# Two-layer hybrid streaming encoder on one core: attention weights of units 2 to 7 turned by VectorE blocks and a round trip through DRAM instead of by TensorE

## What is computed

```python
def swa_mixer(p, sinks, cos, sin):
    q, k, v = split_cols(p, (4 * 64, 2 * 64, 2 * 64))
    ...
    kb, vb = band(kr, km), band(vr, vm)          # 16 meta keys, the previous chunk, the own chunk
    ...
    pr = sink_softmax(jnp.einsum('bcqkgd,bcskd->bckgqs', qr, kb), sink, valid)
    orr = jnp.einsum('bckgqs,bcskd->bcqkgd', pr.astype(v.dtype), vb)
```

## Time and profile before

| | |
|---|---|
| runs | 3054.97, 3055.97, 3060.37 us; median 3055.97 |
| profiled execution, its own time | 3056.32 us |
| span of its trace | 3054.4 us |
| PE busy | 3011.8 us, 99% of the span |
| DVE, ACT, POOL busy | 1529.4, 939.6, 216.8 us |
| DMA | 760.19 MB, mean 249 GB/s |

### The profile page before, as it was taken

The page is one execution under the profiler, slowest core; times in us unless marked ns, Lnnn a source line. Parts: engine busy times, 40 slices in busy tenths (PEclk is TensorE's granted clock), DMA queues, the critical chain, the costliest instruction groups (busy, mean ns, idle before and its releaser), DMA issues.

```text
span 3054.4 us, 64343 instructions
## 1 busy us (share of the span) xinstructions
PE 3011.8 (99%) x27180; PEld 2759.9 (90%) x27180; DVE 1529.4 (50%) x3672; ACT 939.6 (31%) x2381; POOL 216.8 (7%) x319
## 2 busy tenths in 40 slices
PE   8999999999999999999999999999999999999998
PEld 7788778889898899989989899999999999999998
DVE  4345552355633455336554366544566255663562
ACT  3324440134421343124341144303343043421320
POOL 0111010011101110010010101000000000000000
PEclk9999999999999999999999999999999999999999
DMA  7577477788978989888797898986768857787887
GB/s 256 170 205 213 118 208 218 220 237 283 311 236 263 280 273 320 242 259 272 238 313 210 264 276 261 295 284 196 260 205 268 290 178 249 210 267 253 301 302 248
DMA packets 227116, 760.19 MB, mean 249 GB/s; under 512 B 25088, under 2 KB 44672, under 8 KB 226576
## 3 DMA queue, kind: packets, MB, share of 16 engines
q1 hardware_dynamic: 189328, 620.80, 61.6%
q0 software_dynamic: 37504, 135.28, 18.0%
HBM read 744.33 MB, written 136.31 MB: 288 GB/s over the span
## 4 chain that ended last, share of the span: by engine, by line
PE 92%; DMA 3%; DVE 3%; ACT 2%; issue 0%; SPq 0%; ACTq 0%; DVEq 0%
PE psum L1853 29%; PE psum L1306 27%; PE psum L1876 10%; PE psum L1912 8%; PE psum L1443 7%; DMA slots<-in_weights 2%; PE psum L1300 1%; PE psum L1322 1%; PE psum L1621 1%; PE psum L1646 1%; DMA slots<-wsum 1%; PE psum L1633 1%; PE psum L1572 1%; PE psum L1694 1%; PE psum L1803 1%
## 5 line engine op out<-in xcount | busy, mean ns | idle before, releaser
L1306 PE MATMUL psum<-hT,slots 128*128 128x256 f32 (+1 forms) x2880 | 658.9, 387 | 2.8 <-ACT hT L874 2.1
L1306 PEld LDWEIGHTS psum<-hT,slots 128*128 128x128 f32 x2880 | 541.6, 190 | 97.0 <-issue 5.5
L1853 PE MATMUL psum<-tsum,slots 128*128 128x128 f32 (+1 forms) x4928 | 608.0, 277 | 11.6 <-ACT raw L1223 4.9
L1853 PEld LDWEIGHTS psum<-tsum,slots 128*128 128x128 f32 x4928 | 573.1, 191 | 28.6 <-issue 20.2
L1853 PE MATMUL psum<-hT,slots 128*128 128x128 f32 (+1 forms) x3696 | 453.7, 276 | 6.9 <-DMA slots<-in_weights 3.9
L1853 PEld LDWEIGHTS psum<-hT,slots 128*128 128x128 f32 x3696 | 432.6, 192 | 10.1 <-DMA slots<-in_weights 4.9
L1876 PE MATMUL psum<-gT,slots 128*128 128x256 f32 (+1 forms) x1408 | 309.9, 383 | 0.0
L1876 PEld LDWEIGHTS psum<-gT,slots 128*128 128x128 f32 x1408 | 267.1, 190 | 40.9
L1306 PE MATMUL psum<-mixT,slots 128*128 128x256 f32 (+2 forms) x1024 | 226.4, 381 | 1.1 <-DVE hT L2030 1.1
L1306 PEld LDWEIGHTS psum<-mixT,slots 128*128 128x128 f32 x1024 | 194.3, 190 | 29.7 <-issue 1.5
L2030 DVE SCALAR_TENSOR_TENSOR hT<-hT,psum 128x256 f32<-128x256 f32 (+2 forms) x96 | 40.5, 423 | 348.3 <-PE psum L1876 249.7
(11 more groups left out here) (326 smaller groups left out, 3526.6 us busy)
## 6 DMA issues: line engine op xcount, KB each, us to landing
slots<-in_weights SPq DMA_DIRECT2D x667, 512.0 KB, 4.6
slots<-wsum SPq DMA_DIRECT2D x308, 512.0 KB, 4.5
wsum<-in_weights POOLq DMA_DIRECT2D x132, 512.0 KB, 6.7
slots<-wsumi SPq DMA_DIRECT2D x64, 512.0 KB, 4.4
slots<-wsumd SPq DMA_DIRECT2D x64, 512.0 KB, 4.5
wsum<-wsum POOLq DMA_DIRECT2D x44, 512.0 KB, 7.9
wsumi<-in_weights POOLq DMA_DIRECT2D x24, 512.0 KB, 7.5
wsumd<-in_weights POOLq DMA_DIRECT2D x24, 512.0 KB, 9.3
```

Of the source, the lines that this page charges most:

```text
L1306: ins = mm(psum[:, i % 2, :n], lhsT, rhs, start=k == 0, stop=k == len(pairs) - 1)
L1853: ins = mm(dst[:, e * n:(e + 1) * n], w[:, (4 * e + k) * P:(4 * e + k + 1) * P], moving[s][k], start=s in (0, 1, 5) and e == 0 and k == 0, ...
```

## The change

For tiles of 128 queries in units 2 to 7 (`weights_by_blocks`: twelve tiles) TensorE's transposes and ACT's two copies of them are gone. In their place:

- DVE, in the step of the normalisation, turns the weights in blocks of 32 by 32 (`v.transpose`, two instructions, L2669) from `PR` into `PC`, which lies in `sc`. `sc` grows from 832 to 1024 columns, and `PR` has rows of 224 instead of 208 columns.
- SP writes all of `sc` to a DRAM tensor `pdram` (`weights_to_dram`, one DMA of 512 KB with rows of 4 KB), and later reads it back into `PB` with the blocks regrouped by key (`weights_by_keys`, four DMAs of 128 KB, each 32 partitions by 4 pieces of 1 KB). The write is placed where SP has waited for the fourth product behind the one at the normalisation's step, the read where it has waited for the seventh (`PUT_AFTER, GET_AFTER = 4, 7`). The write waits for DVE's blocks (`p_cut`) and for the read before it (`p_in`), the read waits for the write to have landed (`p_out`).
- TensorE's four matmuls with the values read `PB`; they wait for all four reads (`p_in`). They come one step later than before, so a tile takes six lane steps, and the second tile starts at step 15 (unit 4: 17 and 23).
- GpSimd zeroes the last 128 columns of `sc` once, and the space for its DMA descriptors is halved from 2048 to 1024 bytes.

```diff
@@ -114,6 +114,7 @@
 N_IN = len(IN_TILES)
 KH = KF // 2
 DN_BLOCKS = 3
+ALL_TILES = [(u, j) for u in range(NU) for j, _, _ in tiles_of(u)]
 DN_SLOTS = 8 * DN_BLOCKS
 UNIQUE = N_IN + KD + NUP + DN_SLOTS
 
@@ -122,6 +123,22 @@
 RET_PART = ["rq0", "rq1", "rk0", "rk1", "rv0", "rv1", "rg0", "rg1"]
 CONV_PART = ["cc0", "cx0", "cb0", "cc1", "cx1", "cb1"]
 SWA_PART = ["sq0", "sq1", "sk", "sv"]
+
+
+def keys_by_blocks(u, j):
+    return u > 0 and j > 0
+
+
+def weights_by_blocks(u, j):
+    return u > 1 and j > 0
+
+
+def tiles_where(test, nth):
+    return sum(test(*tile) for tile in ALL_TILES[:nth])
+
+
+def tiles_not(test, nth):
+    return nth - tiles_where(test, nth)
 
 
 def input_part(u):
@@ -200,7 +217,25 @@
 
 BLOCKS = all_blocks()
 AT = {key: i for i, key in enumerate(BLOCKS)}
+PUT_AFTER, GET_AFTER = 4, 7
 assert len(AT) == len(BLOCKS)
+
+
+def lane_block(u, step):
+
+    return AT[u - 1, f"us{step // 3}_{2 * (step % 3) + 1}"]
+
+
+def weight_turns():
+
+    out = {}
+    for nth, (u, j) in enumerate(ALL_TILES):
+        if weights_by_blocks(u, j):
+            i, nt, k = [t for t, _, _ in tiles_of(u)].index(j), len(tiles_of(u)), tiles_where(weights_by_blocks, nth)
+            start = 3 * nt + 3 + (5 if nt == 3 else 0) + 6 * (i - (nt == 3))
+            out[lane_block(u, start + 1) + PUT_AFTER] = ("put", k)
+            out[lane_block(u, start + 1) + GET_AFTER] = ("get", k)
+    return out
 
 
 def sum_points(l):
@@ -419,7 +454,8 @@
         wset = sb("wset", 5632)
         Zb = sb("Zb", 256)[:, :].rearrange("p (b t k) -> p b t k", b=2, t=2)
         YW = sb("YW", 768)
-        SC = sb("SC", 4 * WIN)[:, :].rearrange("p (h s) -> p h s", h=4)
+        sc = sb("SC", 1024)
+        SC = sc[:, 0:4 * WIN].rearrange("p (h s) -> p h s", h=4)
         prpt = sb("prpt", 1024 + 4 * CW)
         rS = sb("rS", 256)[:, :].rearrange("p (b t k) -> p b t k", b=2, t=2)
         tab = sb("tab", 4 * CW)[:, :].rearrange("p (k t) -> p k t", k=4)
@@ -442,7 +478,10 @@
         isum = wset[:, 0:16 * (CW // 2)].rearrange("p (j k t) -> p j k t", j=4, k=4)
         dsum = wset[:, 0:4 * KH * P].rearrange("p (j k t) -> p j k t", j=4, k=KH)
 
-        PR = prpt[:, 0:4 * WIN].rearrange("p (h s) -> p h s", h=4)
+        PR = prpt[:, 0:28 * BLOCK].rearrange("p (h s) -> p h s", h=4)
+        PC = sc[:, 0:1024].rearrange("p (q m c) -> p q m c", q=4, m=2)
+        PB = prpt[:, 1024:2048].rearrange("p (b m c) -> p b m c", b=4, m=2)
+        pdram = nc.dram_tensor("pdram", (P, 1024), F32, kind="Internal").ap()
         PT = prpt[:, 1024:2048].rearrange("p (m h s) -> p m h s", m=2, h=4)
         rKt, rVt = prpt[:, 0:256], prpt[:, 256:512]
         rSM = prpt[:, 512:1024].rearrange("p (h s) -> p h s", h=4)
@@ -628,12 +667,27 @@
                 for dst, src in turned(temp("tk", n), temp("sk", n)):
                     sp.dma_start(dst, src).then_inc(S["k_turn"], 16)
 
+            def weights_to_dram(nth):
+
+                sp.wait_ge(S["p_cut"], nth + 1)
+                if nth:
+                    sp.wait_ge(S["p_in"], 64 * nth)
+                sp.dma_start(pdram, sc[:, 0:1024]).then_inc(S["p_out"], 16)
+
+            def weights_by_keys(nth):
+
+                sp.wait_ge(S["p_out"], 16 * (nth + 1))
+                source = pdram.rearrange("(b s) (q c) -> q s b c", b=4, q=4)
+                for q in range(4):
+                    sp.dma_start(PB[BLOCK * q:BLOCK * (q + 1)].rearrange("p b m c -> p b (m c)"), source[q]).then_inc(S["p_in"], 16)
+
             first = C_AT["first_end"]
             load_input(1, sp)
             sp.dma_start(con[:, :first], consts[:, :first]).then_inc(S["in_ident"], 16)
             load_input(0, sp)
             load_input(2, sp)
             sp.dma_start(ln_in_sb[:, :], ln_in).then_inc(S["in_first"], 16)
+            turns = weight_turns()
             for i, (l, which, u, name, q) in enumerate(USES):
                 if i >= SLOTS:
                     _, _, u0, name0, q0 = USES[i - SLOTS]
@@ -647,6 +701,9 @@
                         turn_attention(u0)
                     if name0 == "sk":
                         turn_key(u0)
+                    if name0[:2] == "us" and AT[u0, name0] in turns:
+                        what, k = turns[AT[u0, name0]]
+                        (weights_to_dram if what == "put" else weights_by_keys)(k)
                 if name[:2] == "us":
                     if name[-2:] == "_1" and u == (1, NCH)[l]:
                         sp.wait_ge(S["ws_third"], 16 * (GROUPS * l + int(name[2:-2]) + 1))
@@ -693,6 +750,7 @@
             g.memset(kbuf[:, :, :], 0.0).then_inc(S["init"], 1)
             g.memset(vbuf[:, :, :], 0.0).then_inc(S["init"], 1)
             g.memset(PCp, 1.0).then_inc(S["init"], 1)
+            g.memset(sc[:, 28 * BLOCK:1024], 0.0).then_inc(S["init"], 1)
             g.wait_ge(S["in_con"], 16)
 
             def rwkv(u):
@@ -1178,7 +1236,17 @@
                     act(es[:n_], sk4[:n_], ACT.Exp).then_inc(S["a_es"], 1)
                     yield
                     yield
-                    a.wait_ge(S["a_pt"], nth + 1)
+                    if weights_by_blocks(u, j):
+                        yield
+                        yield
+                        a.wait_ge(S["a_oT"], nth + 1)
+                        for g in range(2):
+                            ins = act(mixT[:, 2 + g, off:off + P].rearrange("p (b s) -> p b s", b=4),
+                                      bank(BX)[:, 0:2 * P].rearrange("p (b g s) -> p g b s", b=4, g=2)[:, g], ACT.Copy)
+                        ins.then_inc(S["a_mix"], 1)
+                        yield
+                        continue
+                    a.wait_ge(S["a_pt"], tiles_not(weights_by_blocks, nth) + 1)
                     for m in range(2 if j else 1):
                         rows_m = min(w - P * m, P)
                         ins = act(PT[:rows_m, m, :, :n_], bank(BX + m).rearrange("p (h s) -> p h s", h=4)[:rows_m, :, :n_],
@@ -1789,14 +1857,27 @@
                     yield
                     yield
                     yield
-                    pe.wait_ge(S["a_pn"], nth + 1)
+                    if weights_by_blocks(u, j):
+                        yield
+                        yield
+                        pe.wait_ge(S["p_in"], 64 * (tiles_where(weights_by_blocks, nth) + 1))
+                        for m in range(2):
+                            rows_m = min(w - P * m, P)
+                            for kv in range(2):
+                                ins = mm(bank(BX)[HD * kv:HD * kv + HD, 0:2 * P].rearrange("p (b c) -> p b c", b=4),
+                                         Vw[:rows_m, b, m, HD * kv:HD * kv + HD],
+                                         PB[:rows_m, :, m, 2 * BLOCK * kv:2 * BLOCK * (kv + 1)], start=m == 0, stop=m == 1)
+                        ins.then_inc(S["a_oT"], 1)
+                        yield
+                        continue
+                    pe.wait_ge(S["a_pn"], tiles_not(weights_by_blocks, nth) + 1)
                     for m in range(2 if j else 1):
                         rows_m = min(w - P * m, P)
                         for h in range(4):
                             ins = transpose(bank(BX + m)[:rows_m, h * P:h * P + n_], PR[:n_, h, P * m:P * m + rows_m], n_)
                     ins.then_inc(S["a_pt"], 1)
                     yield
-                    pe.wait_ge(S["a_ptc"], nth + 1)
+                    pe.wait_ge(S["a_ptc"], tiles_not(weights_by_blocks, nth) + 1)
                     for m in range(2 if j else 1):
                         rows_m = min(w - P * m, P)
                         for kv in range(2):
@@ -2581,8 +2662,16 @@
                     after(k)
                     k = step(v.reciprocal(rden[:n_], den[:n_]))
                     after(k)
-                    tt(PR[:n_, :, :w], PR[:n_, :, :w], rden[:n_, :, None].broadcast_to([n_, 4, w]),
-                       ALU.mult).then_inc(S["a_pn"], 1)
+                    ins = tt(PR[:n_, :, :w], PR[:n_, :, :w], rden[:n_, :, None].broadcast_to([n_, 4, w]), ALU.mult)
+                    if weights_by_blocks(u, j):
+                        after(step(ins))
+                        for m in range(2):
+                            ins = v.transpose(PC[:, 0:4 - m, m].rearrange("p q (h s) -> p q h s", h=4),
+                                              PR[:, :, P * m:P * m + P - BLOCK * m].rearrange("p h (q s) -> p q h s", s=BLOCK))
+                        ins.then_inc(S["p_cut"], 1)
+                        yield
+                    else:
+                        ins.then_inc(S["a_pn"], 1)
                     yield
                     yield
                     yield
@@ -2921,7 +3010,7 @@
     import concourse.bacc as bacc
     from concourse.bass_utils import run_bass_kernel_spmd
 
-    nc = bacc.Bacc("TRN2", target_bir_lowering=False, num_devices=1, dynamic_dma_scratch_size=2048)
+    nc = bacc.Bacc("TRN2", target_bir_lowering=False, num_devices=1, dynamic_dma_scratch_size=1024)
```

(4 more changed lines are left out.)

## The result

| | before | after |
|---|---|---|
| median | 3057.95 us (4 runs, 3054.97 to 3060.37) | 3110.75 us (4 runs, 3107.93 to 3112.03) |
| profiled execution, its own time | 3056.32 us | 3110.43 us |
| span of its trace | 3054.4 us | 3108.6 us |

A forecast was written before the change was run, and what follows sets the result against it. PE, busy 99% of the span, was taken to bound the kernel. 3056.3 - 11.2 - 3.3 - 4 + 1 + 24 + 5.6 = 3068.4 us, predicted as 3068; likeliest case 3057 to 3082, 8 in 10 from 3040 to 3090.

The forecast's parts named there:

- The sign, the place and the mechanism: Slower by 12 us, mainly in units 2 to 5, where POOL's transfers share the DMA engines and the round trip lands late.
- (a) the transposes, -11.2: On PE's path, 0.93 us of transposes goes in each of twelve tiles: -11.2 us.
- (b) ACT's waits, -3.3: Second tiles' exponentials come one step later, so PE's 0.66 us waits for ACT go: -3.3 us, 0 if they only move.
- DVE, ACT's copies, the memset, the descriptor space: nothing: DVE's block transposes, ACT's dropped copies, the start's memset and POOL's halved descriptor space change the time by nothing.
- Write and read in the busy tiles, +24: Seven tiles in units 2 to 5: late write and read cost 24 us, lower end 0, upper end 39.
- draining is certain: Busy tiles: when PE stands, slot loads and POOL's transfers stop and queues drain, so 24 us instead of 38.8.
- a count by mean bandwidth: Busy tiles: 1.05 MB more per tile at 326 GB/s is 3.2 us, or 22.5 us over seven tiles.
- Quiet tiles, +1: Units 6, 7 and unit 4's second tile: write in time, read by a hair; 0.2 us each, five tiles, +1 us.
- The estimate of the room: On PE's timeline per tile, 6.2 us for the write to land and 6.3 us for the read.
- Today's slot waits, -4: Part of PE's present 10.2 us of slot waits, mostly in busy units, is swallowed by the new stops: -4 us.
- (d) the clock, +5.6: TensorE's clock halves after long stops, 1.4 us each in four of seven busy tiles: +5.6 us, ends 0 and 9.8.
- Rival 3, small pieces: The read's 1 KB pieces starve against POOL's 4 KB in all seven busy tiles: 3093 us, chance 0.14.

The follow-up runs named there:

- Experiment 1: The change without the DRAM write and reads, PE waiting for DVE's blocks instead: 3047.47 us, ratio 0.9976 to the kernel before.
- the control: The kernel before with POOL's layer 1 sums moving 64 of 1024 columns and SP loading weight blocks in place of those sums: 3045.67 us, ratio 0.9964.
- experiment 2: The kernel before, with its TensorE transposes, given six lane steps per big tile instead of five: 3055.49 us, ratio 1.0005.
- experiment 7: The change with POOL's layer 1 sums moving 64 of 1024 columns and SP loading weight blocks instead of sums: 3047.47 us, ratio 0.9973 to before.
- experiment 6: The change in units 6 and 7 only: 3050.08 us; also with large read pieces 3050.87, or with seven lane steps 3047.73 us.
- Experiment 3: The change with only the write, nothing read back: 3061.88 us, ratio 1.0024; with only the reads, from a weight block: 3096.17 us, 1.0145.
- Experiment 4: The change with the product with the values three lane steps later: 3082.80 us, ratio 1.0093; with reads also behind the eleventh product: 3065.81 us, 1.0037.
- experiment 5: The change with the 1 KB pieces moved to four writes and one read in 4 KB rows: 3089.30 us, ratio 1.0117 to before.

## Why the prediction was wrong

The sign, the place and the mechanism were right, the size was not: 12 us forecast, 53 measured, outside the range that ended at 3090. The first step that failed is the cut of the busy tiles' waits from 38.8 to 24 us, on the ground that the queues drain while PE stands. Between the traces 42 us are missing from the sum: 11.5 in those tiles' reads, 5 in the quiet ones, 10.5 in the slot waits, 12.9 in the clock and 2 in ACT's and small waits.

- **(a) the transposes, -11.2**: right. Experiment 1's PE is busy 10.5 us less with 3.4 us more at half clock.
- **(b) ACT's waits, -3.3**: the waits went (L1223's 4.9 us became L1291's 1.2), the time did not. L1221's 3.4 us (the same before and in the control's row) became L1289's 4.8, and experiment 2 gains nothing. The step "-3.3 us (0 if the wait only moves)" should have used its bracket; slots were already late.
- **DVE, ACT's copies, the memset, the descriptor space: nothing.** Nearly: SP never waited for DVE's blocks, but PE's two new waits for DVE in unit 4 are 1.7 us. The descriptor space was not tried by itself; no lateness of PE is traced to it, and medians of POOL's own transfers to landing are 6.7 to 9.3 us for the sums (6.7 to 10.6 before).
- **Write and read in the busy tiles, +24**: this failed first. The seven tiles' reads made PE wait 35.5 us against 24, near the upper bound of 38.8. The fall from 38.8 to 24 rested on "draining is certain", which no row showed. POOL's transfers were already placed behind PE's products, but the one in flight, and the slot loads that SP had issued, go on while PE stands. The other reason, a count by mean bandwidth (3.2 us of traffic per tile), says what the engines owe in all and not when one given transfer lands. Rows of landings were the right measure, and their bound should have been taken. That the bound came so near is partly luck, for its parts were off: SP stood 29.8 us in `p_out` against the 13.3 us that the slots' medians gave, for the writes' own landings in units 2 to 5 were 5.2 to 13.0 us; and the four read issues took 1.3 us from first to last in seven tiles and up to 2.3 in the others, not 1.95.
- **Quiet tiles, +1**: 6.0 us, of which 4.45 is one tile, unit 6's second. Its last read landed 8.7 us after its issue, and the three slot loads issued ahead of the reads took 6.9 to 9.4 us, with no transfer of POOL's in flight; in unit 7's second tile the same loads took 5.1 to 5.6 and the read 5.2. The same tile has the longest read wait of experiment 7 too, 2.8 us, and in experiment 6 the longest of all read waits was 1.4. What slows this stretch is open. The estimate of the room was good: unit 7's two reads took 6.5 and 6.6 us from first issue to last landing, against 6.3 of room, and PE waited about 0.2 and 0.69 us.
- **Today's slot waits, -4**: the wrong sign, +6.5. The step counted only the lateness that a stop of PE covers, and put the trip's own traffic and SP's stops at nothing there. Experiment 3's writes alone, with SP never stopped, add 12.1 us of slot waits. A stop of SP comes on top: while SP stands in `p_out`, no slot load goes out, and the slots are late after PE has gone on. Experiment 4 prices it: 17 us between the form with that wait and the one without. How the 6.5 us divide between the two is not shown.
- **(d) the clock, +5.6**: +18.5. All seven late reads of the busy tiles paid, not four of seven, and with unit 6's and two other stops there were ten spells against one before. The nine more cost 2.1 us each on the mean and lasted up to 10.2 us, against 1.4 us from the single spell of 3.4 us. The profile before showed one such stop. The Trainium skill (TensorE: Matmul & The Clock Gate, "HAM oscillation") has a wait for DMA between bursts throttle again each time, and here the trace agrees in all eight late reads over 2 us. It is no rule for every short stop: in experiment 7 read waits of 2.32 and 2.37 us had no spell behind them and one of 1.77 us had, and in experiment 5 a slot wait of 2.71 us had none.
- **Rival 3, small pieces**, came nearest in time (3093, still 18 us short), and by luck: its waits of 51.1 us for reads and writes were 9.5 too long, its clock was 8.7 too little, and it took 10 us off the slot waits where 6.5 came on. Its cause is worth about 1.1 us a tile on the read (experiment 5).

By the recorded sum with the failed terms replaced by what the trace shows: 3056.3 - 11.2 + 41.6 + 6.5 + 18.5 - 1.2 = 3110.5, the profiled execution's own time up to rounding.

## What to carry to other kernels

Price a new transfer by the landings of its neighbours in the same stretch, at their medians and their worst, and keep that bound: mean bandwidth tells what the engines carry and not when one transfer is there. A wait for a landing on the queue that prefetches weights costs twice, once for its own consumer and once as late prefetches; place the reader so far behind the writer that the queue never stands (here eleven products instead of seven). That alone did not pay here: the form was still 0.37% slower than before. Use such a trip only where the DMA engines have room, and add the half clock after the stops of the matmul engine, here 2.1 us for each spell.

## What the runs showed of the hardware

- A DMA's landing depended on its company far more than on its size. In units 6 and 7 of the change a write of 512 KB landed in 3.7 to 4.3 us and a read of 128 KB in 2.9 to 5.2, one at 8.7 apart; in units 2 to 5 the writes took 5.2 to 13.0 and the reads 3.1 to 11.0. Over all tiles the round trip's DMAs had a median of 3.9 us with POOL's large transfers taken out and 5.6 us with them, and a worst of 7.3 and 13.0 us.
- The last of four equal DMAs landed latest after its issue in every one of the twelve tiles, sometimes long after the others; why is not shown. The four reads at 1947 us, issued over 1.3 us (first and last start in the row), landed between 3.1 and 9.7 us after issue, and the product waits for the last:

```profile
L682 SPq DMA_DIRECT2D prpt<-pdram x4: 325/432/432, 1947.4 to 1948.7; - x4
...
DMA to landing us min/median/max: 3.1/5.8/9.7
```

- Taking away 37 MB of POOL's traffic, of 760 MB in all, gave the kernel before 11 us (ratio 0.9964): its slot waits fell from 10.2 to 2.1 us. They had looked like noise; all but 1.6 us of them lay in units 2 to 5, the very units where the change put its transfers onto engines with a share of 0.96 to 1.03.
